# Hybrid decoder layer, gate/up stage: chunk 7's parts made at chunks 0 and 1 with one accumulating DMA, and the next block's sums put ahead of the mixing

## The chip, the cores and the metric

One NeuronCore of a Trainium2 chip runs the kernel alone. The metric is the device time of one execution in microseconds (us), lower is better. PE is TensorE, DVE is VectorE, ACT is ScalarE, POOL is GpSimd and SP is SyncE, whose queue issues most loads.

## The reference, cut to what matters

One layer on 256 tokens of width 2048: token mixing by head groups, then a dense SwiGLU feed-forward part and a final norm. All weights are float32. The part in question is the last but one line:

```python
    x = x + y @ w_out
    h = rms_norm(x, ffn_norm)
    return x + (jax.nn.silu(h @ w_gate) * (h @ w_up)) @ w_down
```

w_gate and w_up are 2048 x 5632 each, w_down is 5632 x 2048.

## The kernel before, in words

**Products.** Each float32 operand is split into a high part (rounded to float32r by a ScalarE copy) and a low part (VectorE: value less high part). A product is three matmuls: high by high, high by low, low by high. Each matmul has a 128x128 stationary tile and 512 columns.

**Chunks.** The weights are worked off in chunks of 1 MB, 128 partitions by four blocks of 512 columns. The gate/up stage has 11 blocks (FS) of 8 chunks (FB): a block makes 512 columns of gate and of up for both token halves, which gather in four PSUM banks. Chunks 1, 3, 6 and 7 are plain: 24 matmuls. Chunks 0, 2, 4 and 5 (SUMS) use a Winograd form of 2 by 2 blocks with seven products instead of eight: 21 matmuls. For it VectorE makes four sums of blocks, t_sum (three instructions, L1231 to L1236), ScalarE their high parts t_hi (L749) and VectorE their low parts t_lo (L1244), besides w_hi and w_lo of three blocks. There are two buffers of t_sum, t_hi and t_lo, used in turn. The seven products gather in seven banks; behind chunk 5, the last of them, the extra banks are mixed into the four: ScalarE copies one (L864), VectorE makes three sums (mix_sums) and then adds to two banks (mix_banks half 0) and subtracts from the other two (half 1). PE resumes into these banks with chunk 7.

**Ring and order.** All chunks but chunk 7 go through a ring of four raw buffers; w_lo is written over raw. SP loads a chunk when the one four places before it is used (chunk_used). ScalarE and VectorE prepare a chunk AHEAD = 3 chunks before PE takes it, in an order written out by hand in ffn(): at step p the chunk p + 3 is prepared. Both engines run that list in order, so a wait in it holds all that is behind it.

**Chunk 7 (BY_DMA).** It goes round the ring. SP loads it into d_raw (L407) when the block before is done (in block 0: when x is saved and normed, behind the load of chunk 5). ScalarE copies it to d_hi (L845) and writes -d_hi over it as d_lo (L848), at step 2, in block 0 at step 3. POOL then adds the weights from HBM to d_lo by an accumulating DMA (L480), which gives the low part without VectorE. d_raw and d_lo are the same memory.

**Hidden values.** At step 7 ScalarE applies Silu to the gate banks and VectorE multiplies by up (L1417). PE transposes the result at the next block's chunks 0 and 1 (hidden_turn, L1533), both times into bank 3, and ScalarE keeps each half in hid (keep_hidden, L818). The second transposition waits for the first half to be kept, the last side of chunk 1 for the second.

**Down stage.** 44 chunks (2 x DQ), with the same forms; the first three are prepared within the last gate/up block (down_hi, down_lo), with the hidden values' high and low parts xo_hi and xo_lo and four sums of them in sf.

Of the kernel before, what the change touches and what calls it, by code (L numbers as in the profile page):

```python
# [7 lines left out]
F32 = mybir.dt.float32  # L8
# [116 lines left out]
def build(nc, t):  # L125
    with ExitStack() as ctx:
# [45 lines left out]
        sf = at("sf", 144 * K, [4, P])  # L172
# [259 lines left out]
        def _(pool):  # L432
# [53 lines left out]
        def _(act):  # L486
# [327 lines left out]
            def keep_hidden(i, banks):  # L814

                for u in range(2):
                    act.wait_ge(turned, i * 2 + (u - 1))
                    nc.scalar.activation(hid[:, bass.ds(i * 4 + (2 * u - 4), 2), :].rearrange("p a b -> p (a b)"),  # L818
                                         bank[banks[u]], ACT.Copy).then_inc(hid_kept, 1)
# [5 lines left out]
            def down_hi(m):  # L825

                r, q = ring(DN0 + m), m % DQ
                slot = r % 4
                act.wait_ge(raw_in[slot], 16 * (r // 4 + 1))
                blocks = slice(1, 4) if q in DSUMS else slice(0, 4)  # L830
                nc.scalar.activation(w_hi[slot][:, blocks, :], raw[slot][:, blocks, :], ACT.Copy).then_inc(hi_ready, 1)  # L831
                act.wait_ge(hid_kept, 2 * FS if q >= DQ - 2 else 2 * FS - 2)
                nc.scalar.activation(xo_hi[m % 4][:, 0:4, :].rearrange("p a b -> p (a b)"),
                                     hid[:, 2 * q:2 * q + 2, :].rearrange("p a b -> p (a b)"), ACT.Copy).then_inc(xo_split, 1)
                if q in DSUMS:
# [4 lines left out]
                    nc.scalar.activation(xo_hi[m % 4][:, 4:8, :], sf[:], ACT.Copy).then_inc(xo_split, 1)  # L840

            def prep_apart(i):

                act.wait_ge(d_in, 16 * (i + 1))
                nc.scalar.activation(d_hi[:], d_raw[:], ACT.Copy).then_inc(d_hi_made, 1)  # L845
                act.wait_ge(d_hi_made, i + 1)
                for half in (slice(0, 2), slice(2, 4)):
                    nc.scalar.activation(d_lo[:, half, :], d_hi[:, half, :].bitcast(F32), ACT.Copy,  # L848
                                         scale=-1.0).then_inc(negated, 1)
# [51 lines left out]
            for m in range(2 * DQ):  # L901
                h, q = divmod(m, DQ)
                if m == 0:
                    keep_hidden(FS, (3, 3))
                    act.wait_ge(chunk_used, DN0)
                    act.dma_start(fnorm[:], t["final_norm"].partition_broadcast(P)).then_inc(fnorm_in, 16)
# [28 lines left out]
        def _(dve):  # L935
# [279 lines left out]
            def prep_lo(i, q, parts="sl"):  # L1215
# [11 lines left out]
                if "s" in parts:  # L1227
                    dve.wait_ge(raw_in[slot], 16 * (r // 4 + 1))
                    if p == SUMS[-1]:
                        dve.wait_ge(chunk_used, i * FB + (FF0 + SUMS[1] + 1))  # L1230
                    nc.vector.tensor_tensor(t_sum[s][:, 0:2, :], raw[slot][:, 1:3, :],  # L1231
# [4 lines left out]
                    nc.vector.tensor_tensor(t4, t2, b21, ALU.add).then_inc(sum_step, 1)  # L1236
                if "l" not in parts:
                    return
                dve.wait_ge(sum_step, i * (3 * NS) + (3 * done + 3))
                dve.wait_ge(hi_ready, r + 1)  # L1240
                nc.vector.tensor_tensor(w_lo[slot][:, 1:4, :], raw[slot][:, 1:4, :], w_hi[slot][:, 1:4, :].bitcast(F32),  # L1241
                                        ALU.subtract)
# [5 lines left out]
            for n in range(G0, FF0):  # L1248
# [12 lines left out]
                if n + AHEAD >= FF0:  # L1261
                    prep_lo(0, n + AHEAD - FF0, "s" if n == FF0 - 1 else "sl")
                elif n != MID:
                    low(n + AHEAD)
# [89 lines left out]
            def down_lo(m):  # L1354
# [3 lines left out]
                x = hid[:, 2 * q:2 * q + 2, :].rearrange("p a (t c) -> p (a t) c", t=TOK)  # L1358
                if q not in DSUMS:
# [3 lines left out]
                    dve.wait_ge(xo_split, m + down_sums_before(m) + 1)  # L1363
                    nc.vector.tensor_tensor(xo_lo[m % 4][:, 0:4, :], x, xo_hi[m % 4][:, 0:4, :].bitcast(F32),
# [6 lines left out]
                dve.wait_ge(raw_in[slot], 16 * (r // 4 + 1))  # L1371
                nc.vector.tensor_tensor(t_sum[s % 2][:, 0:2, :], raw[slot][:, 1:3, :],
                                        b12.unsqueeze(1).to_broadcast([P, 2, COLS]), ALU.add).then_inc(sum_step, 1)
                dve.wait_ge(sum_step, before + 1)
                nc.vector.tensor_tensor(t2, t1, b22, ALU.add).then_inc(sum_step, 1)
                dve.wait_ge(sum_step, before + 2)
                nc.vector.tensor_tensor(t4, t2, b21, ALU.add).then_inc(sum_step, 1)
                s3_s1, n2, s4 = sf[:, 0:2, :], sf[:, 2, :], sf[:, 3, :]
                dve.wait_ge(xo_split, m + s + 1)
                if s:  # L1380
                    dve.wait_ge(xo_made, DSUMS[(s - 1) % DNS] + DQ * ((s - 1) // DNS) + 1)
                nc.vector.tensor_tensor(s3_s1, x[:, 0:4:3, :], x[:, 1:2, :].to_broadcast([P, 2, P]),
                                        ALU.subtract).then_inc(xo_step, 1)
                dve.wait_ge(xo_step, 3 * s + 1)
                nc.vector.tensor_tensor(n2, sf[:, 1, :], x[:, 0, :], ALU.add).then_inc(xo_step, 1)
                dve.wait_ge(xo_step, 3 * s + 2)
                nc.vector.tensor_tensor(s4, x[:, 2, :], n2, ALU.subtract).then_inc(xo_step, 1)
                dve.wait_ge(sum_step, before + 3)
                dve.wait_ge(hi_ready, r + 1)
                nc.vector.tensor_tensor(w_lo[slot][:, 1:4, :], raw[slot][:, 1:4, :], w_hi[slot][:, 1:4, :].bitcast(F32),  # L1390
                                        ALU.subtract)
                nc.vector.tensor_tensor(xo_lo[m % 4][:, 0:4, :], x, xo_hi[m % 4][:, 0:4, :].bitcast(F32), ALU.subtract)
# [7 lines left out]
            def ffn(i, first=False, last=False):  # L1400
                for p in range(FB):
                    if p == 0 and first:
                        for j, u in enumerate(UNITS[FF0]):
                            dve.wait_ge(unit_filled, INDEX[u] + 1)
                            split_pair_lo(u, late_bank[j])
                        prep_lo(i, 2, "l")
# [13 lines left out]
                    if last and p + AHEAD >= FB:  # L1420
                        down_lo(p + AHEAD - FB)
                        if p == SUMS[-1]:
                            mix_banks(i, 1, i * FB + (FF0 + 7))
                    elif p == SUMS[-1]:
                        prep_lo(i, p + AHEAD, "s")
                        mix_banks(i, 1, i * FB + (FF0 + 7))
                        prep_lo(i, p + AHEAD, "l")
                    elif p + AHEAD != BY_DMA:
                        prep_lo(i, p + AHEAD)
# [61 lines left out]
        def _(pe_):  # L1491
# [375 lines left out]
            def ffn(i, first=False):  # L1867
                for p in range(FB):
                    if p == BY_DMA:
                        pe_.wait_ge(lo_added, 32 * (i + 1))  # L1870
# [173 lines left out]
```

## Time and profile before

| | us |
|---|---|
| median of 3 runs | 1151.44 (1151.28 to 1152.26) |
| profiled execution | 1152.47 |
| its span | 1150.7 |
| PE busy | 1098.2 (95%) |
| DVE busy | 911.0 (79%) |
| ACT busy | 653.4 (57%) |
| POOL busy | 69.8 (6%) |
| mean granted clock of PE | 0.984 |

The span is the profiled execution from its first to its last instruction. Matmuls are pipelined: one is 0.39 us long in the trace, but they start 0.227 us apart. The granted clock is a share of 2.4 GHz. The gate/up stage starts at about 387 us and the down stage at 912 us of the span.

### The profile page before, as it was taken

What the parts mean: (1) busy time and instruction counts of PE and PEld (TensorE: products, weight loads), DVE (VectorE), ACT (ScalarE), POOL (GpSimd) and SP (SyncE); (2) the same over time, 40 slices, a digit from 0 to 9 for tenths busy, and PEclk for the clock granted to TensorE, in tenths of its full rate; (3) what the DMA queues carried; (4) which work ended last, traced back from release to release, by engine and by line L of the source; (5) the groups of instructions that cost most, each with busy time, mean ns of one, the idle gap of its engine ahead of it and who ended that gap; (6) DMA issues with size and microseconds to landing.
All of it is one profiled execution on the core that took longest, in us unless ns stands there. A gap on an engine that the chain in (4) does not pass through costs nothing.

```text
span 1150.7 us, 12406 instructions
## 1 busy us (share of the span) xinstructions
PE 1098.2 (95%) x5094; PEld 906.2 (79%) x5094; DVE 911.0 (79%) x858; ACT 653.4 (57%) x650; POOL 69.8 (6%) x66
## 2 busy tenths in 40 slices
PE   9999999999999989899798998989989899999997
PEld 6888889977888768687686877868778688888886
DVE  7789577745666988778877788977888799999995
ACT  7567466657645655464545645545555566565653
POOL 0087000000000000000000000000000000000000
PEclk9999999999999999999999999999999999999999
DMA  8765535643555784665747667566576766565562
GB/s 330 283 227 191 195 104 162 200 146 111 169 193 184 248 266 165 200 202 200 219 146 203 204 187 242 187 186 209 191 219 195 229 234 200 201 197 206 194 208 110
DMA packets 52025, 228.56 MB, mean 199 GB/s; under 512 B 4480, under 2 KB 10368, under 8 KB 31744
## 3 DMA queue, kind: packets, MB, share of 16 engines
q1 hardware_dynamic: 47936, 213.84, 54.6%
q0 software_dynamic: 3168, 11.54, 5.6%
q10 hardware_dynamic: 864, 2.39, 0.6%
q8 instruction: 40, 0.66, 0.2%
q14 instruction: 17, 0.14, 0.0%
HBM read 223.56 MB, written 4.19 MB: 198 GB/s over the span
## 4 chain that ended last, share of the span: by engine, by line
PE 64%; DVE 10%; ACT 10%; DMA 9%; issue 6%; POOL 1%; SPq 0%; DVEq 0%; ACTq 0%
PE ps L1641 43%; DMA d_lo<-in_w_gu 8%; PE ps L1494 5%; PE ps L1496 5%; PE ps L1495 5%; ACT t_hi L749 4%; DVE w_lo L1221 3%; DVE t_sum L1231 2%; ACT w_hi L741 2%; PE ps L1533 2%; ACT d_hi L845 2%; DVE t_sum L1236 1%; DVE t_sum L1234 1%; ACT d_lo L848 1%; POOL d_lo L480 1%
## 5 line engine op out<-in xcount | busy, mean ns | idle before, releaser
L749 ACT ACTIVATE t_hi<-t_sum 128x2048 fp32r<-128x2048 f32 x44 | 84.4, 1918 | 190.2 <-DVE t_sum L1236 190.2
L1641 PE MATMUL ps<-w_hi,xp_hi 128*128 128x512 f32 x396 | 157.4, 397 | 4.2 <-DVE w_lo L1221 3.6
L948 DVE TENSOR_TENSOR w_lo<-raw,w_hi 128x2048 fp32r<-128x2048 f32 (+2 forms) x42 | 87.3, 2077 | 86.6 <-ACT w_hi L492 86.6
L1641 PE MATMUL ps<-w_lo,xp_hi 128*128 128x512 f32 x396 | 154.5, 390 | 0.0
L1641 PE MATMUL ps<-w_hi,xp_lo 128*128 128x512 f32 x396 | 154.4, 390 | 0.0
L831 ACT ACTIVATE w_hi<-raw 128x2048 fp32r<-128x2048 f32 (+1 forms) x44 | 79.1, 1799 | 76.2 <-DMA raw<-in_w_dn 76.1
L1221 DVE TENSOR_TENSOR w_lo<-raw,w_hi 128x2048 fp32r<-128x2048 f32 x33 | 75.5, 2289 | 51.4 <-ACT w_hi L741 51.4
L1641 PE MATMUL ps<-w_hi,xo_hi 128*128 128x512 f32 x292 | 113.9, 390 | 0.0
L1641 PE MATMUL ps<-w_hi,xo_lo 128*128 128x512 f32 x292 | 113.6, 389 | 0.0
L1641 PE MATMUL ps<-w_lo,xo_hi 128*128 128x512 f32 x292 | 113.6, 389 | 0.0
L1244 DVE TENSOR_TENSOR t_lo<-t_sum,t_hi 128x2048 fp32r<-128x2048 f32 x44 | 100.8, 2290 | 6.4 <-ACT t_hi L749 6.4
L492 ACT ACTIVATE w_hi<-raw 128x2048 fp32r<-128x2048 f32 (+2 forms) x42 | 73.0, 1738 | 50.4 <-DMA raw<-in_w_out 25.6
L1641 PEld LDWEIGHTS ps<-w_hi,xp_hi 128*128 128x128 f32 x396 | 74.3, 188 | 23.5 <-DVE w_lo L1221 7.9
L1641 PEld LDWEIGHTS ps<-w_hi,xp_lo 128*128 128x128 f32 x396 | 74.3, 188 | 15.9
L1641 PEld LDWEIGHTS ps<-w_lo,xp_hi 128*128 128x128 f32 x396 | 74.4, 188 | 14.4
L1361 DVE TENSOR_TENSOR w_lo<-raw,w_hi 128x2048 fp32r<-128x2048 f32 x32 | 73.2, 2286 | 12.3 <-ACT w_hi L831 12.3
L1641 PE MATMUL ps<-d_hi,xp_hi 128*128 128x512 f32 x88 | 42.2, 480 | 37.9 <-DMA d_lo<-in_w_gu 37.6
L1241 DVE TENSOR_TENSOR w_lo<-raw,w_hi 128x1536 fp32r<-128x1536 f32 x44 | 77.3, 1756 | 1.1
L1641 PE MATMUL ps<-t_hi,xp_hi 128*128 128x512 f32 x176 | 68.5, 389 | 0.4 <-DVE xp_lo L1190 0.4
L1641 PE MATMUL ps<-t_hi,xp_lo 128*128 128x512 f32 x176 | 68.5, 389 | 0.0
L1641 PE MATMUL ps<-t_lo,xp_hi 128*128 128x512 f32 x176 | 68.5, 389 | 0.0
L745 ACT ACTIVATE w_hi<-raw 128x1536 fp32r<-128x1536 f32 x44 | 65.2, 1481 | 5.2 <-DMA raw<-in_w_gu 4.9
(289 smaller groups left out, 2529.6 us busy)
## 6 DMA issues: line engine op xcount, KB each, us to landing
raw<-in_w_gu SPq DMA_DIRECT2D x77, 1024.0 KB, 4.9
raw<-in_w_dn SPq DMA_DIRECT2D x44, 1024.0 KB, 4.8
raw<-in_w_i SPq DMA_DIRECT2D x21, 1024.0 KB, 4.9
raw<-in_w_out SPq DMA_DIRECT2D x16, 1024.0 KB, 5.1
raw<-in_w_in SPq DMA_DIRECT2D x12, 1024.0 KB, 5.2
d_raw<-in_w_gu SPq DMA_DIRECT2D x11, 1024.0 KB, 4.8
d_lo<-in_w_gu POOLq DMA_DIRECT2D x22, 512.0 KB, 8.2
raw<-in_w_in SPq DMA_DIRECT2D x8, 576.0 KB, 3.8
```

The source lines that it names most:

```text
L492: nc.scalar.activation(w_hi[n % 4][:, 0:k, 0:c], raw[n % 4][:, 0:k, 0:c], ACT.Copy).then_inc(hi_ready, 1)
L745: nc.scalar.activation(w_hi[slot][:, 1:4, :], raw[slot][:, 1:4, :], ACT.Copy).then_inc(hi_ready, 1)
L749: nc.scalar.activation(t_hi[s % 2][:], t_sum[s % 2][:], ACT.Copy).then_inc(tops_hi, 1)
L831: nc.scalar.activation(w_hi[slot][:, blocks, :], raw[slot][:, blocks, :], ACT.Copy).then_inc(hi_ready, 1)
L948: nc.vector.tensor_tensor(w_lo[n % 4][:, 0:k, 0:c], raw[n % 4][:, 0:k, 0:c], w_hi[n % 4][:, 0:k, 0:c].bitcast(F32), ALU.subtract).then_inc ...
L1221: nc.vector.tensor_tensor(w_lo[slot][:], raw[slot][:], w_hi[slot][:].bitcast(F32), ALU.subtract).then_inc(lo_ready, 1)
L1241: nc.vector.tensor_tensor(w_lo[slot][:, 1:4, :], raw[slot][:, 1:4, :], w_hi[slot][:, 1:4, :].bitcast(F32), ALU.subtract)
L1244: nc.vector.tensor_tensor(t_lo[s][:], t_sum[s][:], t_hi[s][:].bitcast(F32), ALU.subtract).then_inc(lo_ready, 1)
L1361: nc.vector.tensor_tensor(w_lo[slot][:], raw[slot][:], w_hi[slot][:].bitcast(F32), ALU.subtract).then_inc(lo_ready, 1)
L1494: nc.tensor.matmul(out, hi, w_h, start=start, stop=False)
L1495: nc.tensor.matmul(out, hi, w_l, start=False, stop=False)
L1641: mm = nc.tensor.matmul(out, x, wt, start=start and j + m == 0, stop=stop and 3 * j + m == n - 1, skip_group_check=resumed)
```

## The change

It moves the preparation of chunk 7. ScalarE makes d_hi at step 0 (block 0: step 1) and the negated copy one step later, between w_hi and t_hi of the chunk prepared there, in one instruction instead of two. The accumulating DMA is one of 1 MB instead of two of 512 KB. The second half of hid is kept after w_hi of chunk 3 instead of ahead of it.

At step 5, VectorE makes the next block's chunk 0 sums first, then mix_sums, then w_lo of its three blocks, then both mixing instructions, then t_lo. Before, the order was mix_sums, mixing half 0, sums, mixing half 1, w_lo, t_lo. ScalarE's w_hi of next chunk 0 comes at step 4 instead of 5. The last block does the same with down chunk 0, whose sums of hidden values go to a buffer of their own, sf_first. The new waits are on chunk 4 being used (for the t_sum buffer) and, in down chunk 2, on chunk 0's xo_lo.

```diff
+        sf_first, sf_later = at("sf_first", 132 * K, [4, P]), at("sf", 144 * K, [4, P])
...
             for i in range(FS):
-                for half in range(2):
-                    pool.wait_ge(negated, 2 * i + half + 1)
-                    pool.dma_start(d_lo[:, 2 * half:2 * half + 2, :].rearrange("p a b -> p (a b)"),
-                                   w_gu[:, FB * i + BY_DMA, 2 * COLS * half:2 * COLS * (half + 1)],
-                                   accum_op=ALU.add).then_inc(lo_added, 16)
+                pool.wait_ge(negated, i + 1)
+                pool.dma_start(d_lo[:].rearrange("p a b -> p (a b)"), w_gu[:, FB * i + BY_DMA, :],
+                               accum_op=ALU.add).then_inc(lo_added, 16)
...
                     elif p == 0:
-                        keep_hidden(i, (3, 3))
+                        keep_hidden(i, (0,))
...
-                    if last and p + AHEAD >= FB:
-                        down_hi(p + AHEAD - FB)
-                    elif p + AHEAD != BY_DMA:
-                        prep_hi(i, p + AHEAD)
-                    if p == (3 if first else 2):
-                        prep_apart(i)
+                    q = p + AHEAD
+                    if q == BY_DMA:
+                        if last:
+                            down_hi(0, "b")
+                        else:
+                            prep_hi(i, FB, "b")
+                    elif q == FB:
+                        if last:
+                            down_hi(0, "t")
+                        else:
+                            prep_hi(i, FB, "t")
+                    elif last and q > FB:
+                        down_hi(q - FB)
+                    elif q in SUMS:
+                        prep_hi(i, q, "b")
+                        if p == (2 if first else 1):
+                            apart_negated(i)
+                        prep_hi(i, q, "t")
+                    else:
+                        prep_hi(i, q)
                     if first and p == 0:
                         root(nx2, 1, D)
+                    elif p == 0:
+                        keep_hidden(i, (1,))
+                    if p == (1 if first else 0):
+                        apart_hi(i)
...
                     if p == SUMS[-1]:
+                        ahead = (lambda parts: down_lo(0, parts)) if last else (lambda parts: prep_lo(i, FB, parts))
+                        ahead("s")
                         mix_sums(i)
+                        ahead("w")
                         mix_banks(i, 0, None)
+                        mix_banks(i, 1, i * FB + (FF0 + 7))
+                        ahead("l")
```

Here "b" is w_hi of the raw blocks, "t" is t_hi, "s" the sums, "w" w_lo of three blocks and "l" t_lo.

## Rows read from the trace of the kernel before

**Rows 1.** Windows from transposition to transposition: length, PE, PEld, DVE, ACT, POOL busy, clock, DMA.
```profile
586.46:634.50 48.04, 43.99 (x190) 35.55 (x188) 39.24 (x31) 25.45 (x20) 1.73 (x2) 0.96 0.64 197
...
681.57:726.95 45.38, 42.39 (x190) 34.41 (x189) 38.65 (x31) 24.93 (x20) 1.76 (x2) 1.00 0.67 209
...
sum 475.52, PE 437.13 PEld 353.53 DVE 393.78 ACT 256.99 POOL 17.42; mean PE 43.71 PEld 35.35 DVE 39.38 ACT 25.70 POOL 1.74
```
**Rows 2.** Waits of PE, 420 to 1140 us: us in total, times, longest.
```profile
PE ps L1641 <- DMA d_lo<-in_w_gu: 37.6, 11, 5.6
PE ps L1641 <- DVE w_lo L1221: 3.6, 10, 0.4
```
**Rows 3.** Timeline of PE: start, length; 581.69 is chunk 0, 613.08 chunk 6.
```profile
581.69 0.39 PE L1641 MATMUL ps<-w_hi,xp_hi 128*128 128x512 f32 x1
...
586.46 0.60 PE L1533 MATMUL ps<-ident,gate 128*128 128x128 f32 x4
...
588.29 0.60 PE L1533 MATMUL ps<-ident,gate 128*128 128x128 f32 x4
...
613.08 0.50 PE L1641 MATMUL ps<-w_hi,xp_hi 128*128 128x512 f32 x1 [0.36 <-DVE w_lo L1221]
```
**Rows 4.** Timeline of ACT in the same block.
```profile
585.33 1.92 ACT L749 ACTIVATE t_hi<-t_sum 128x2048 fp32r<-128x2048 f32 x1 [4.12 <-DVE t_sum L1236]
587.15 0.58 ACT L818 ACTIVATE hid<-ps 128x512 f32<-128x512 f32 x1
...
589.42 1.91 ACT L741 ACTIVATE w_hi<-raw 128x2048 fp32r<-128x2048 f32 x1
...
596.26 1.92 ACT L749 ACTIVATE t_hi<-t_sum 128x2048 fp32r<-128x2048 f32 x1 [3.19 <-DVE t_sum L1236]
...
604.96 1.90 ACT L845 ACTIVATE d_hi<-d_raw 128x2048 fp32r<-128x2048 f32 x1
```
**Rows 5.** The view of the tile d_lo: landing of the accumulating DMAs.
```profile
DMA to landing us min/median/max: 5.7/8.2/12.3
```
**Rows 6.** Timeline of POOL: the second DMA of a block.
```profile
616.84 0.86 POOL L480 DMA_DIRECT2D d_lo<-in_w_gu  x1 [7.72 <-issue]
```
**Rows 7.** The view of the tile d_raw: landing of its loads.
```profile
DMA to landing us min/median/max: 4.7/4.8/6.9
```
**Rows 8.** Timeline of DVE in the same block.
```profile
581.96 0.75 DVE L1417 SCALAR_TENSOR_TENSOR gate<-ps,stats,gate 128x512 f32<-128x512 f32 x1 [0.61 <-PE ps L1641]
582.63 1.21 DVE L1231 TENSOR_TENSOR t_sum<-raw 128x1024 f32<-128x1024 f32 x1
...
587.28 2.29 DVE L1244 TENSOR_TENSOR t_lo<-t_sum,t_hi 128x2048 fp32r<-128x2048 f32 x1 [0.19 <-ACT t_hi L749]
...
612.94 0.68 DVE L1332 TENSOR_TENSOR mix<-mix,ps 128x512 f32<-128x512 f32 x1
...
614.91 0.69 DVE L1337 TENSOR_TENSOR mix<-ps,mix 128x512 f32<-128x512 f32 x1
616.17 1.23 DVE L1347 TENSOR_TENSOR ps<-ps,mix 128x1024 f32<-128x1024 f32 x1 [0.57 <-PE ps L1641]
```
**Rows 9.** The page's DMA issues: the raw loads, KB each, median us to landing.
```profile
raw<-in_w_gu SPq DMA_DIRECT2D x77, 1024.0 KB, 4.9
```
**Rows 10.** The same view from 660 to 663 us: one load beside an accumulation.
```profile
raw<-in_w_gu SPq DMA_DIRECT2D x1, 1024.0 KB, 8.9
```
**Rows 11.** Timeline of DVE in the last gate/up block, down chunk 0.
```profile
898.49 1.22 DVE L1372 TENSOR_TENSOR t_sum<-raw 128x1024 f32<-128x1024 f32 x1
...
904.33 2.28 DVE L1394 TENSOR_TENSOR t_lo<-t_sum,t_hi 128x2048 fp32r<-128x2048 f32 x1
```
**Rows 12.** Timeline of SP's queue: the first load into d_raw.
```profile
399.88 0.34 SPq L407 DMA_DIRECT2D d_raw<-in_w_gu  x1
```
**Rows 13.** Timeline of ACT in block 0: w_hi of chunk 5, ahead of d_hi.
```profile
405.52 1.47 ACT L745 ACTIVATE w_hi<-raw 128x1536 fp32r<-128x1536 f32 x1
```
**Rows 14.** The page's first line.
```profile
span 1150.7 us, 12406 instructions
```

More of the change, by code:

```diff
@@ L839, in down_hi, with apart_hi, apart_negated @@
                     act.wait_ge(xo_step, 3 * (s + 1))
-                    nc.scalar.activation(xo_hi[m % 4][:, 4:8, :], sf[:], ACT.Copy).then_inc(xo_split, 1)
-            def prep_apart(i):
+                    nc.scalar.activation(xo_hi[m % 4][:, 4:8, :], (sf_later if m else sf_first)[:], ACT.Copy).then_inc(xo_split, 1)
+            def apart_hi(i):
                 act.wait_ge(d_in, 16 * (i + 1))
                 nc.scalar.activation(d_hi[:], d_raw[:], ACT.Copy).then_inc(d_hi_made, 1)
+            def apart_negated(i):
                 act.wait_ge(d_hi_made, i + 1)
-                for half in (slice(0, 2), slice(2, 4)):
-                    nc.scalar.activation(d_lo[:, half, :], d_hi[:, half, :].bitcast(F32), ACT.Copy,
-                                         scale=-1.0).then_inc(negated, 1)
+                nc.scalar.activation(d_lo[:], d_hi[:].bitcast(F32), ACT.Copy, scale=-1.0).then_inc(negated, 1)
             def ffn(i, first=False, last=False):
@@ L1236, in prep_lo @@
                     nc.vector.tensor_tensor(t4, t2, b21, ALU.add).then_inc(sum_step, 1)
+                if "w" in parts or "l" in parts:
+                    dve.wait_ge(sum_step, i * (3 * NS) + (3 * done + 3))
+                    dve.wait_ge(hi_ready, r + 1)
+                if "w" in parts:
+                    nc.vector.tensor_tensor(w_lo[slot][:, 1:4, :], raw[slot][:, 1:4, :], w_hi[slot][:, 1:4, :].bitcast(F32),
+                                            ALU.subtract)
                 if "l" not in parts:
                     return
[L1239 to L1242, printed above, removed]
                 dve.wait_ge(tops_hi, i * NS + (done + 1))
@@ L1358, in down_lo @@
                 x = hid[:, 2 * q:2 * q + 2, :].rearrange("p a (t c) -> p (a t) c", t=TOK)
+                sf = sf_later if m else sf_first
                 if q not in DSUMS:
@@ L1370, in down_lo @@
                 before = 3 * (NS * FS + s)
[L1371 to L1377, printed above, removed]
@@ L1386, in down_lo @@
[L1386 to L1392, printed above, removed]
+                if "s" in parts:
+                    dve.wait_ge(raw_in[slot], 16 * (r // 4 + 1))
+                    if m == 0:
+                        dve.wait_ge(chunk_used, DN0 - FB + SUMS[2] + 1)
+                    nc.vector.tensor_tensor(t_sum[s % 2][:, 0:2, :], raw[slot][:, 1:3, :],
+                                            b12.unsqueeze(1).to_broadcast([P, 2, COLS]), ALU.add).then_inc(sum_step, 1)
+                    dve.wait_ge(sum_step, before + 1)
+                    nc.vector.tensor_tensor(t2, t1, b22, ALU.add).then_inc(sum_step, 1)
+                    dve.wait_ge(sum_step, before + 2)
+                    nc.vector.tensor_tensor(t4, t2, b21, ALU.add).then_inc(sum_step, 1)
+                    s3_s1, n2, s4 = sf[:, 0:2, :], sf[:, 2, :], sf[:, 3, :]
+                    dve.wait_ge(hid_kept, 2 * FS - 2)
+                    if s:
+                        dve.wait_ge(xo_made, DSUMS[(s - 1) % DNS] + DQ * ((s - 1) // DNS) + 1)
+                    nc.vector.tensor_tensor(s3_s1, x[:, 0:4:3, :], x[:, 1:2, :].to_broadcast([P, 2, P]),
+                                            ALU.subtract).then_inc(xo_step, 1)
+                    dve.wait_ge(xo_step, 3 * s + 1)
+                    nc.vector.tensor_tensor(n2, sf[:, 1, :], x[:, 0, :], ALU.add).then_inc(xo_step, 1)
+                    dve.wait_ge(xo_step, 3 * s + 2)
+                    nc.vector.tensor_tensor(s4, x[:, 2, :], n2, ALU.subtract).then_inc(xo_step, 1)
@@ new lines, in down_lo @@
+                if "w" in parts:
+                    dve.wait_ge(sum_step, before + 3)
+                    dve.wait_ge(hi_ready, r + 1)
+                    nc.vector.tensor_tensor(w_lo[slot][:, 1:4, :], raw[slot][:, 1:4, :], w_hi[slot][:, 1:4, :].bitcast(F32),
+                                            ALU.subtract)
+                    dve.wait_ge(xo_split, m + s + 1)
+                    nc.vector.tensor_tensor(xo_lo[m % 4][:, 0:4, :], x, xo_hi[m % 4][:, 0:4, :].bitcast(F32), ALU.subtract)
@@ L1393, in down_lo @@
+                if "l" not in parts:
+                    return
                 dve.wait_ge(tops_hi, NS * FS + s + 1)
@@ L1419, in ffn @@
                                                            op0=ALU.mult, op1=ALU.mult).then_inc(hid_made, 1)
-                    if last and p + AHEAD >= FB:
+                    if p + AHEAD > FB and last:
                         down_lo(p + AHEAD - FB)
[L1422 to L1428, printed above, removed]
+                    elif p + AHEAD not in (BY_DMA, FB):
                         prep_lo(i, p + AHEAD)
```

48 lines of the change are left out of this document (22 added, 26 removed).

## The prediction

> **What bounds the kernel now.** I read the page first, then the waits of TensorE (PE), then the execution cut at PE's first transposition of each gate/up block, then the order of instructions on PE, ScalarE and VectorE in one block. PE is the engine to watch: from 440 to 916 us it is busy 437.1 of 475.5 us [rows 1], and of the time it is idle behind the start of the gate/up stage 37.6 us in 11 waits is one wait, that for the accumulating DMA into d_lo, once a block, ahead of chunk 7; another 3.6 us in ten waits is for w_lo of chunk 6 [rows 2]. The reader is to see two prices in the table by block. A block takes 47.55 us on average (475.52 / 10). In the block from 681.57 PE is granted its full clock, 2.4 GHz, and is busy 42.4 us; in the one from 586.46 the mean granted clock is 0.96, because PE runs at 1.2 GHz for a few microseconds behind its stall, and it is busy 44.0 us for the same 190 instructions [rows 1]. So a stall is paid once as idle time and, in most blocks, once more as clock.
>
> What would a block take without any stall? Chunk 0 (21 matmuls) runs from 581.69 to 586.46, 0.227 us per matmul; the two groups of transpositions add some 0.45 us each, since 588.29 - 586.46 = 1.83 us holds one of them and six matmuls [rows 3]. Four chunks of 21 matmuls and four of 24 make 180 x 0.227 + 0.9 = 41.75 us. That is the floor: 5.8 us under today's block.
>
> VectorE is not far behind: 39.4 us busy a block [rows 1]. Whatever the change gives, it can't pass some 40 us a block, and the order of VectorE's work decides what is left over. So I walk one block with the new order. T = 0 is the start of chunk 7; chunk 0 starts at 5.44, the transpositions at 10.2 and 12.04, chunks 2 to 6 at 16.55, 21.3, 26.75, 31.5 and 36.3, the next chunk 7 at 41.75 if nothing waits.
>
> **The change, part by part.**
>
> *Chunk 7's parts earlier.* Today d_hi and the two halves of d_lo are made from 604.96 on, behind t_hi of chunk 5 [rows 4], and the DMAs issue there. The halves land 5.7 to 12.3 us behind their issue, and in some blocks POOL gets the second one out 7.72 us after the first [rows 5, 6]: 13 to 14.3 us (7.72 + 0.87 + 5.7) from the first issue to the last landing; with the average stall of 3.4 us PE wants them some 10 us after it. In the new order d_raw is wanted from 14.7 and was issued at 5.5, landing 4.8 us later [rows 7]. ScalarE: hid's first half to 12.4 (below), w_hi of chunk 3 (1.9) to 14.2, hid's second half to 14.8, d_hi to 16.6, w_hi of chunk 4 (1.5) to 18.0, then the negation in one instruction to 19.9. The last one takes the place of an idle wait, the 3.19 us before t_hi at 596.26 [rows 4], though not quite: t_sum is complete at 19.1, so t_hi and t_lo of chunk 4 come 0.8 us later than they could. Chunk 4 starts at 26.75 and t_lo ends at 24.0, so that costs nothing. The one DMA of 1 MB issues at 20.2. No row shows a 1 MB accumulation. I bound it by 8.2 us (a median half) from below and 14.3 us (both halves with the longest issue gap) from above [rows 5, 6], and take 12.3. It lands at 32.5, at worst 34.5, against 42 when PE asks: 7 us of cover. The stall of 3.4 us (37.6 / 11) goes entirely, the slow clock behind it (437.13 / 10 - 42.4 = 1.3 us a block) too, and the 0.36 us for chunk 6 goes as w_hi of chunk 6 no longer stands behind d_hi and the negation. The semaphore count (16 instead of 32) costs nothing.
>
> *hid's second half behind w_hi of chunk 3.* PE's second transposition only needs the first half; the second half is needed for the last side of chunk 1, at 15.7. It is kept at 14.8: 0.9 us of cover, cost nothing.
>
> *The first half of hid, where the next stall is.* With chunk 7 no longer late, VectorE has nothing to wait for there. The second mixing instruction starts 0.43 us behind PE's end of chunk 6 (that is T; the same semaphore latency as the 0.57 us of [rows 8]) and takes 1.2; t_lo of the next chunk 0 and w_lo of the next chunk 1 take 2.2 each (2.29 less the overlap with the next instruction); the gate products take 0.67 each (581.96 to 582.63) and so sums of chunk 2 start at 7.3; t_hi follows 2.70 later (582.63 to 585.33), at 10.0; hid's first half starts 1.82 later and lasts 0.58, to 12.4 [rows 4, 8]. PE asks at 12.04. So PE waits 0.45 us with latency, once a block; all later chunk times move by it: chunk 3 at 21.8, 4 at 27.2, 5 at 32.0, 6 at 36.7, next 7 at 42.2.
>
> *Next chunk 0's sums ahead of the mixing.* In the old order mix_sums (612.94 to 615.6, 2.66 us) and the first mixing instruction come first [rows 8]. In the new one, the chain ahead of chunk 7 is: w_lo of chunk 6, sums of next 0 (2.70), mix_sums (2.66), three blocks of w_lo (587.28 - 0.19 - 585.33 = 1.76 at most, 1.67 with overlap), first mixing instruction (1.23 and 0.1 latency). That is 8.35 us from the start of the sums to PE's release. The sums wait for the raw load, which SP issues when chunk 3 is used, at 27.3, so it depends on its landing, and here the earlier accumulation costs something: it now runs from 20.2 to 32.5, over the loads of chunk 6 (issued 21.9) and next 0 (27.3). A raw load takes 4.9 us in the median, but one issued inside an accumulation took 8.9 [rows 9, 10]. With chunk 6 at the midpoint of 6.3 and 8.9 its w_lo is through at 33.6. For next 0, bounds 4.9 and 8.9, I take 7.2, since the accumulation ends 5 us into it: 34.5. Then PE is released at 34.5 + 8.35 = 42.85 instead of 42.2. With 4.9 it would be released at 41.9 (VectorE then starts at 33.6) and wait for nothing; with 8.9 at 44.5. I take a block of 42.9 us.
>
> The trace's 8.9 us is the row on which this stands. The Trainium skill (DMA: Bandwidth & Descriptors, Queues, rings and completion order) says that a DMA engine takes turns between the queues that have work for it, packet by packet, whoever issued it; that speaks against moving the accumulation to where loads are on the path. By that rule a load may take twice its 4.9 us while an accumulation runs; the trace, with 8.9, agrees.
>
> *Last block.* There the sums carry those of hid as well, and w_lo the split of xo: 898.49 to 904.33 is 5.84 us where another block needs 587.28 - 0.19 - 582.63 = 4.46 [rows 8, 11]. 1.4 us more: 44.3. The added buffer sf_first and the wait of xo_lo in chunk 2 of the down stage cost nothing: the writer is ahead in VectorE's own order. From 916 us on PE never waits for long and I take this stage as it is.
>
> *Block 0.* Its d_raw load is issued at 399.9 and lands 6.9 us later, at 406.8 [rows 7, 12]. ScalarE now waits for it ahead of w_hi of chunk 5, which ran at 405.52 [rows 13]: d_hi to 408.6, w_hi to 410.1, negation to 412.0, t_hi to 413.9, t_lo to 416.2 against 414.8. PE starts chunk 5 some 1.4 us later. What it saves is the average stall and clock, 3.4 + 1.3 = 4.7: gain 3.3.
>
> **Sum.** 9 x 42.9 + 44.3 = 430.4, against 475.5: 45.1 us less, and 3.3 of block 0: 48.4. The profiled execution took 1152.5 us (its span 1150.7 [rows 14]), which gives 1104.1; the median of the runs is 1.0 us lower, so 1103.
>
> **Rivals.**
> A, nothing waits: the loads land in under 6 us and hid's first half in time. 41.75 a block and 43.1 for the last: 418.9 + block 0's 3.3 to 4.7: 61 us less, 1091. For it: my chains miss by only 0.45 and 0.65 us. Against: VectorE has 2 us of slack a block and several waits to take from it.
> B, the loads are the new wait: both take 8.9 us. Chunk 6's raw at 31.7, w_hi 33.6, w_lo 35.8, release at 44.2; next 0's at 8.9, release 44.5. Ten blocks at 44.5 and 1.4: 446.4, 29 + 3 = 32 less: 1119. For it: 8.9 is in the trace; against: the accumulation is over when the second load is half through. By the turns between queues of the Trainium skill (same page and section), a load twice as long as 4.9 us would make it 45.4 a block and 1128, an estimate; the 8.9 stays the bound of the trace.
> C, slower than before: the 1 MB accumulation lands so late that PE waits for it again. It issues at 20.2 and is wanted at 42.2; today's block is 5.8 us longer than the floor, so it decides only from about 27 us after its issue. Halves took at most 14.3 together, with the gap of 7.7 added twice 22. At 30 us a block would be 50 and the time some 1175.
> D, the change brings nothing: a new wait as long as the old one. In B's chain that takes a load of 11.9 us for next 0 (27.3 + 11.9 + 8.35 = 47.5) in each block; no load of before is known to take that. 1150.
>
> **Chances.** My forecast (1097 to 1109) 0.52, A 0.2, B 0.2, D 0.04, C 0.04. The range for 8 in 10 leaves a piece of A and the outer half of B: 1090 to 1116. Measurement tells 0.2% (2.3 us) from no change: faster 0.94, same 0.02, slower 0.04.
>
> **What would show it.** Right: no wait of PE for the DMA into d_lo; one DMA a block issued some 20 us behind chunk 7's start; granted clock 1.00 in all blocks; blocks of 42 to 43.5 us; a wait of PE under 1 us at the second transposition, on hid; one under 1 us ahead of chunk 7, on VectorE's mixing instruction; block 0's chunk 5 later by 1.4 us. Wrong: blocks over 44 us, raw loads landing in over 9 us with VectorE waiting for them ahead of the sums; or a granted clock under 1.00, which small new stalls would have to cause.

## The result, and the profile after

The changed kernel takes 1103.47 us in the median of four runs (1102.71 to 1107.73) against 1151.85 us for the kernel before in the same comparison; the ratio is 0.9584, 95% interval 0.9556 to 0.9612. The forecast was 1103. The profiled execution is the slowest of the four, 1107.73 us with a span of 1105.2, so what follows is up to 5 us on the slow side. Its mean granted clock is 0.995, that of the other three 0.998 to 0.999; over 1105 us that makes 3 to 4 us, an estimate, and so most of the difference.

The windows from transposition to transposition, cut as in [rows 1]; the columns are the same.
```profile
483.14:526.13 42.99, 42.02 (x189) 34.50 (x188) 38.98 (x31) 25.27 (x19) 0.86 (x1) 1.00 0.68 220
526.13:568.26 42.13, 42.02 (x190) 34.49 (x189) 38.90 (x31) 25.09 (x19) 0.89 (x1) 1.00 0.70 224
568.26:611.51 43.25, 42.03 (x189) 34.49 (x188) 39.16 (x31) 25.44 (x19) 0.87 (x1) 1.00 0.68 219
...
653.54:697.24 43.70, 41.99 (x190) 34.46 (x189) 39.23 (x31) 25.50 (x19) 0.86 (x1) 1.00 0.68 216
697.24:739.38 42.14, 42.02 (x189) 34.49 (x188) 38.94 (x31) 25.12 (x19) 0.88 (x1) 1.00 0.70 225
...
825.24:870.76 45.52, 43.63 (x189) 35.63 (x188) 41.23 (x35) 28.40 (x24) 0.86 (x1) 0.96 0.66 212
sum 430.69, PE 422.03 PEld 345.97 DVE 392.90 ACT 256.15 POOL 8.69; mean PE 42.20 PEld 34.60 DVE 39.29 ACT 25.61 POOL 0.87
```
Ten blocks take 430.7 us instead of 475.5. The granted clock is 1.00 in all of them but the last. But they are not equal: from the third on, a block of 42.1 us is followed by one of 43.2 to 43.7.

The waits of PE from 400 to 1100 us (us in total, times, longest) answer to [rows 2]:
```profile
PE ps L1672 <- DVE ps L1369: 8.3, 6, 1.9
PE ps L1672 <- DVE t_lo L1266: 3.0, 1, 3.0
```
The 37.6 us for the accumulating DMA and the 3.6 us for w_lo of chunk 6 are gone. In their place stand waits for VectorE's mixing ahead of chunk 7 (8.3 us in six) and one in block 0 for t_lo of chunk 5 (3.0 us).

The landings of the accumulating DMA and of d_raw, from the views of the two tiles, answer to [rows 5, 7]:
```profile
DMA to landing us min/median/max: 8.5/9.1/10.7
```
```profile
DMA to landing us min/median/max: 4.7/4.9/8.2
```
One DMA of 1 MB lands in about 9 us, less than the 12.3 us that I took, and far ahead of PE.

Where is the new wait made? First ScalarE's timeline, in a block in which PE waited:
```profile
573.82 1.49 ACT L743 ACTIVATE w_hi<-raw 128x1536 fp32r<-128x1536 f32 x1
575.19 1.92 ACT L849 ACTIVATE d_lo<-d_hi 128x2048 fp32r<-128x2048 f32 x1
576.99 1.91 ACT L747 ACTIVATE t_hi<-t_sum 128x2048 fp32r<-128x2048 f32 x1
...
588.81 1.92 ACT L739 ACTIVATE w_hi<-raw 128x2048 fp32r<-128x2048 f32 x1 [3.04 <-DMA raw<-in_w_gu]
```
Then VectorE's from there, and PE's chunk 7:
```profile
590.76 2.29 DVE L1239 TENSOR_TENSOR w_lo<-raw,w_hi 128x2048 fp32r<-128x2048 f32 x1 [2.66 <-ACT w_hi L739]
592.97 1.22 DVE L1251 TENSOR_TENSOR t_sum<-raw 128x1024 f32<-128x1024 f32 x1
...
595.56 0.68 DVE L1354 TENSOR_TENSOR mix<-mix,ps 128x512 f32<-128x512 f32 x1
...
598.14 1.75 DVE L1261 TENSOR_TENSOR w_lo<-raw,w_hi 128x1536 fp32r<-128x1536 f32 x1
599.81 2.36 DVE L1369 TENSOR_TENSOR ps<-ps,mix 128x1024 f32<-128x1024 f32 x2
```
```profile
601.18 0.47 PE L1672 MATMUL ps<-d_hi,xp_hi 128*128 128x512 f32 x1 [1.22 <-DVE ps L1369]
```
The reader is to see an unbroken chain. ScalarE waits 3.04 us for the raw load of chunk 6, w_hi starts at 588.81, and from there w_lo, sums, mix_sums, w_lo and mixing follow without a gap to PE's release at 601.18: 12.4 us. The block before has the same chain from 545.57 to 557.93, also 12.4 us, with PE hardly waiting. The difference is the load of chunk 6. In the block before it was issued at 537.46 and took 8.1 us, in the block shown it was issued at 579.59 and took 9.2 us.

### The profile page after: what moved, and what is told of

It reads as the page before. It is cut to its first block, busy times and chain, and to the rows that moved or that the text cites. A ratio compares the mean times of both kernels' runs of the same rounds, so it can differ in the third digit from the quotient of the medians.

```text
span 1105.2 us, 12406 instructions
## 1 busy us (share of the span) xinstructions
PE 1083.0 (98%) x5094; PEld 898.8 (81%) x5094; DVE 909.5 (82%) x858; ACT 652.5 (59%) x639; POOL 57.4 (5%) x55
## 3 DMA queue, kind: packets, MB, share of 16 engines
q0 software_dynamic: 1584, 11.54, 5.6%
## 4 chain that ended last, share of the span: by engine, by line
PE 82%; DMA 6%; DVE 5%; issue 3%; ACT 3%; SPq 0%; DVEq 0%; ACTq 0%
PE ps L1672 61%; PE ps L1525 5%; PE ps L1527 5%; PE ps L1526 5%; DMA raw<-in_w_gu 5%; PE ps L1564 2%; ACT w_hi L739 1%; DMA d_raw<-in_w_gu 1%; DVE mix L1356 1%; DVE t_sum L1251 1%; DVE ps L1369 1%; PE ps L1612 1%; PE ps L1789 1%; PE ps L1790 1%; PE ps L1791 1%
## 5 line engine op out<-in xcount | busy, mean ns | idle before, releaser
L1384 DVE TENSOR_TENSOR w_lo<-raw,w_hi 128x2048 fp32r<-128x2048 f32 x32 | 73.2, 2288 | 14.4 <-ACT w_hi L830 14.3
L739 ACT ACTIVATE w_hi<-raw 128x2048 fp32r<-128x2048 f32 x33 | 63.0, 1909 | 26.0 <-DMA raw<-in_w_gu 26.0
```

The costliest lines, as they stand in the source:

```text
L739: nc.scalar.activation(w_hi[slot][:], raw[slot][:], ACT.Copy).then_inc(hi_ready, 1)
L1384: nc.vector.tensor_tensor(w_lo[slot][:], raw[slot][:], w_hi[slot][:].bitcast(F32), ALU.subtract).then_inc(lo_ready, 1)
```

## The experiments

Every kernel was compared with the kernel before on the same chip; a ratio is to that kernel, with its 95% interval. The changed kernel was measured in one of these comparisons only. Where another kernel is set against it, that goes by the two ratios, and where their intervals overlap the difference is not secure.

**Only VectorE's old order.** The changed kernel with the order of step 5 put back:
```diff
-                        ahead("s")
                         mix_sums(i)
-                        ahead("w")
                         mix_banks(i, 0, None)
+                        ahead("s")
                         mix_banks(i, 1, i * FB + (FF0 + 7))
-                        ahead("l")
+                        ahead("wl")
```


> The changed kernel with VectorE's old order at step 5 (mix_sums, mixing half 0, sums of next chunk 0, mixing half 1, w_lo, t_lo); all else of the change stays. Theory of the prediction (VectorE has only some 2 us of slack a block once PE no longer waits, so its order decides): mix_sums waits for chunk 5, the sums then push t_lo of the next chunk 0 and the first half of hid back by 2 to 3 us, PE waits for t_lo ahead of chunk 0 or at the second transposition, blocks of 44.5 to 45.5 us, 1120 to 1130 us. Rival (only chunk 7's earlier parts matter, the order is free): 1102 to 1106 us.

Measured: 1125.89 us, ratio 0.977 (0.9746 to 0.9794). Blocks of 44.66 us, all alike. Its waits of PE:
```profile
PE ps L1563 <- ACT hid L816: 16.4, 10, 1.6
PE ps L1671 <- DVE t_lo L1266: 9.6, 11, 2.1
```
Time and blocks are as expected. Both waits that the theory names are there, 0.75 us ahead of each chunk 0 and 1.64 us at each second transposition. So the new order is worth 22 us once the rest of the change is in.

**Only the new order.** Chunk 7's parts as before at step 2, in two halves, and both halves of hid kept ahead of w_hi of chunk 3; the core of the edit:
```diff
-                        if p == (2 if first else 1):
-                            apart_negated(i)
...
-                    elif p == 0:
-                        keep_hidden(i, (1,))
-                    if p == (1 if first else 0):
-                        apart_hi(i)
+                    if p == (3 if first else 2):
+                        apart_hi(i)
+                        apart_negated(i)
```


> The changed kernel with chunk 7's parts where they were (step 2, block 0 step 3), two halves, and hid's halves kept together: only the new order of sums and mixing is left of the change. Theory: PE waits for the accumulating DMA as before, blocks of 47 to 48 us, 1148 to 1153 us. Rival (the order brings a part by itself): under 1140 us.

Measured: 1148.48 us, ratio 0.9965 (0.995 to 0.9981). As the theory has it, PE still waits 31.2 us in ten waits for the DMA. Alone, the order is worth 4 us, 0.35%: the longer wait covers what it gives.

**Only one DMA.** The kernel before with one negation and one DMA, at the old place:
```diff
-                for half in range(2):
-                    pool.wait_ge(negated, 2 * i + half + 1)
-                    pool.dma_start(d_lo[:, 2 * half:2 * half + 2, :].rearrange("p a b -> p (a b)"),
-                                   w_gu[:, FB * i + BY_DMA, 2 * COLS * half:2 * COLS * (half + 1)],
-                                   accum_op=ALU.add).then_inc(lo_added, 16)
+                pool.wait_ge(negated, i + 1)
+                pool.dma_start(d_lo[:].rearrange("p a b -> p (a b)"), w_gu[:, FB * i + BY_DMA, :],
+                               accum_op=ALU.add).then_inc(lo_added, 16)
```


> The kernel before with one negation and one accumulating DMA of 1 MB, at the old place. Theory as predicted (1 MB lands some 12 us after its issue, so the early place is what removes the wait): it issues near 609 in the block of the rows, lands near 621 against 618.9 wanted, PE waits 2.5 us a block, 1135 to 1145 us. Rival (the changed kernel's trace shows 1 MB landing in 8.5 to 10.7 us, so one DMA nearly suffices at the old place): wait under 1 us, 1105 to 1122 us.

Measured: 1134.57 us, ratio 0.9851 (0.9823 to 0.9878). The time falls just under the range of the theory, by other waits than it named:
```profile
PE ps L1637 <- DMA d_lo<-in_w_gu: 17.2, 11, 2.4
PE ps L1529 <- ACT hid L816: 8.7, 8, 1.6
PE ps L1637 <- DVE w_lo L1217: 2.7, 10, 0.3
```
The DMA lands in 9.4 to 11.8 us (median 11.0), so PE waits 1.6 us for it in the mean instead of 3.4. In eight of the blocks it then waits up to 1.6 us at the second transposition, which the longer stall had hidden. A third of the whole gain comes from this edit alone, and not all of it is waiting: PE's busy time fell from 1098.2 to 1089.2 us while its mean granted clock rose from 0.984 to 0.996. That is 9 of the 19.6 us by which the span fell.

**One DMA and the new order, at the old place.** The changed kernel with the edit of "only the new order", but one negation and one DMA.

> The changed kernel with chunk 7's parts at the old place (step 2, block 0 step 3) but one negation and one DMA; hid's halves kept together. It tells what the early place adds where the order and the single DMA are there. Theory: PE waits 0.7 to 2.4 us for the DMA as with the single DMA alone, but not at the second transposition; blocks of 43.2 to 44.5 us, 1112 to 1122 us. Rival (the early place is not needed any more): 1105 us or under.

Measured: 1134.07 us, ratio 0.9851 (0.9833 to 0.9869): both theory and rival missed. The order adds nothing to the single DMA. Its waits of PE, and ScalarE's timeline of one block:
```profile
PE ps L1669 <- DVE ps L1366: 22.5, 9, 3.9
PE ps L1669 <- DMA d_lo<-in_w_gu: 5.0, 2, 2.6
```
```profile
549.20 1.90 ACT L844 ACTIVATE d_hi<-d_raw 128x2048 fp32r<-128x2048 f32 x1
551.13 1.92 ACT L849 ACTIVATE d_lo<-d_hi 128x2048 fp32r<-128x2048 f32 x1
552.95 1.90 ACT L739 ACTIVATE w_hi<-raw 128x2048 fp32r<-128x2048 f32 x1
```
PE's wait ahead of chunk 7 is no longer put down to the DMA but to the mixing, some 2.3 us a block and 3.9 us in the last. w_hi of chunk 6 stands behind d_hi and the negation on ScalarE, which take 3.75 us; VectorE waits 3.26 us for it at 554.88, and the same chain of sums and mixing runs late. With this order the early place does two things: it hides the DMA, and it takes 3.75 us of ScalarE's work from ahead of w_hi of chunk 6.

**Two halves at the new place.** The changed kernel with two negations and two DMAs of 512 KB, the diff of "only one DMA" read backwards, in the changed kernel.

> The changed kernel with two negations and two accumulating DMAs of 512 KB, at the new place. If only the landing counts: the halves are all landed some 14 us behind the first issue (about 34 of T), 7 us ahead of PE; no wait for them, and the time within 3 us of 1103.5, unless the longer traffic delays the raw loads of chunk 6 and next chunk 0 further: then blocks of 43.5 to 44.5 us and 1108 to 1118 us. Rival (one DMA is needed to hide it at all): PE waits for the DMA again, over 1120 us.

Measured: 1107.8 us, ratio 0.9624 (0.9595 to 0.9653). PE doesn't wait for the DMA, which settles the rival; its waits for the mixing are 11.7 us in nine instead of 8.3 in six, and the first nine blocks average 43.24 us instead of 42.80. The time lies between the two that were expected, within 3 us of 1103.5 and 1108 to 1118. The intervals of this ratio and of the changed kernel's overlap, so the 4 us between them are not secure, and whether the longer traffic costs anything stays open.

**No accumulation.** POOL waits for the negation and only counts the semaphore up; chunk 7's low part lacks the weights.
```diff
                 pool.wait_ge(negated, i + 1)
-                pool.dma_start(d_lo[:].rearrange("p a b -> p (a b)"), w_gu[:, FB * i + BY_DMA, :],
-                               accum_op=ALU.add).then_inc(lo_added, 16)
+                pool.sem_inc(lo_added, 16)
```


> The changed kernel without the accumulating DMA: POOL only counts the semaphore up, so chunk 7's low part lacks the weights (-d_hi alone); that part of the computation is left out. Theory (the accumulation's traffic delays the raw load of chunk 6, from which w_hi, w_lo, sums, mix_sums, w_lo and mixing follow in 12.4 us to PE's release at chunk 7): that load lands in about 5 us instead of 8 to 9, no wait at chunk 7, all blocks near 42.1, 1092 to 1096 us. Rival (VectorE's list itself is too long, the load is incidental): the waits at chunk 7 stay, 1101 to 1104 us.

Measured: 1095.15 us, ratio 0.9505 (0.9481 to 0.9528). Two of its windows:
```profile
524.99:566.97 41.98, 41.96 (x189) 34.49 (x188) 39.06 (x31) 25.13 (x19) 0.00 (x0) 1.00 0.59 200
818.91:861.37 42.46, 42.24 (x189) 34.41 (x188) 41.06 (x35) 28.68 (x24) 0.00 (x0) 1.00 0.59 203
```
The first nine blocks take 41.98 to 42.00 us each; the unevenness is gone. The waits of VectorE from 440 to 860 us, first of the changed kernel, then of this one:
```profile
DVE w_lo L1239 <- ACT w_hi L739: 21.8, 10, 3.1
DVE t_lo L1266 <- ACT t_hi L747: 9.8, 30, 0.6
DVE t_sum L1251 <- DMA raw<-in_w_gu: 0.3, 1, 0.3
```
```profile
DVE ps L1368 <- PE ps L1671: 13.4, 9, 1.5
DVE t_lo L1265 <- ACT t_hi L746: 9.8, 30, 0.6
```
With the accumulation, VectorE loses 21.8 us in ten waits for w_hi of chunk 6 and, but for 0.2 us, never waits for PE: its list, with these waits in it, is the bound. Without the accumulation they are gone and VectorE waits for PE. The raw load of chunk 6, which took 8.1 and 9.2 us in the two blocks above, takes 4.9 here in the one block read. So the accumulation's traffic costs the changed kernel some 8 us. The edit frees every load of it, but chunk 6's is the only one for which VectorE had lost more than 0.3 us.

**The first mixing instruction ahead of w_lo.** PE's wait at chunk 7 would lose the 1.67 us of w_lo from its chain:
```diff
                         mix_sums(i)
-                        ahead("w")
                         mix_banks(i, 0, None)
+                        ahead("w")
                         mix_banks(i, 1, i * FB + (FF0 + 7))
```


> The changed kernel with the first mixing instruction ahead of w_lo of next chunk 0 instead of behind it. Theory (PE's wait at chunk 7 is the chain from chunk 6's raw load, 12.4 us, of which w_lo takes 1.67): the chain is 10.7 us, the waits of 1.2 to 1.9 us at chunk 7 shrink to 0 to 0.2, blocks of 42.0 to 42.2 us, the last block 2 us shorter: 1093 to 1097 us. Rival (the second mixing instruction, pushed behind w_lo, is then late for the third side of chunk 7, or t_lo late for chunk 0): waits there of 1 us or more, 1101 us or over.

Measured: 1102.63 us, ratio 0.9585 (0.956 to 0.961): no gain that can be told. The waits of PE moved:
```profile
PE ps L1564 <- ACT hid L816: 5.5, 8, 1.1
PE ps L1672 <- DVE t_lo L1266: 1.6, 1, 1.6
PE ps L1672 <- DVE ps L1369: 0.6, 3, 0.2
```
The waits at chunk 7 shrink as the theory has it, but what VectorE has lost to the late load comes back at the second transposition, up to 1.1 us; neither theory nor rival had named this place, though the time is in the rival's range. VectorE's list is unbroken from w_lo of chunk 6 to the sums of the next chunk 2, on which hid waits; only the order within it changed. The last block of the profiled execution is 2.7 us shorter (42.81 instead of 45.52).

**The negation ahead of w_hi of chunk 4.** The accumulating DMA issues 1.2 to 1.4 us earlier behind the transposition.
```diff
-                        prep_hi(i, q, "b")
-                        if p == (2 if first else 1):
+                        if p == 1 and not first:
                             apart_negated(i)
+                        prep_hi(i, q, "b")
```


> The changed kernel with the negation (and so the accumulating DMA) ahead of w_hi of chunk 4 instead of behind it, 1.4 us earlier; block 0 as it is. Theory (VectorE loses 21.8 us in ten waits for w_hi of chunk 6, whose raw load is slowed by the accumulation; a part of the accumulation's traffic is moved out of that load's way): these waits shrink to 8 to 15 us in all, 1098 to 1101 us. Rival (the traffic in flight is the same and the queues share anew; or w_lo of chunk 4 comes 1 us later and VectorE loses there what it gains): 1102 to 1105 us.

Measured: 1108.67 us, ratio 0.9623 (0.9601 to 0.9645): slower than both expected, though the interval overlaps the changed kernel's. The gain of the theory did not come. VectorE's wait for w_hi of chunk 6 grew to 24.2 us and a new one of 8.0 us in ten came for w_hi of chunk 4. The accumulation now took 10.4 to 11.8 us to land. Moved earlier by this much, it is not out of the loads' way.

**Chunk 6 in halves.** w_hi and w_lo of chunk 6 are made in two halves each, so that VectorE starts 0.9 us sooner:
```diff
+                if p == 6:
+                    nc.scalar.activation(w_hi[slot][:, 0:2, :], raw[slot][:, 0:2, :], ACT.Copy).then_inc(half6_hi, 1)
+                    nc.scalar.activation(w_hi[slot][:, 2:4, :], raw[slot][:, 2:4, :], ACT.Copy).then_inc(hi_ready, 1)
+                    return
...
+                if p == 6:
+                    dve.wait_ge(half6_hi, i + 1)
+                    nc.vector.tensor_tensor(w_lo[slot][:, 0:2, :], raw[slot][:, 0:2, :],
+                                            w_hi[slot][:, 0:2, :].bitcast(F32), ALU.subtract)
+                    dve.wait_ge(hi_ready, r + 1)
+                    nc.vector.tensor_tensor(w_lo[slot][:, 2:4, :], raw[slot][:, 2:4, :],
+                                            w_hi[slot][:, 2:4, :].bitcast(F32), ALU.subtract).then_inc(lo_ready, 1)
+                    return
```


> The changed kernel with w_hi and w_lo of chunk 6 made in two halves each, so that VectorE starts on the first half 0.9 us earlier. The accumulation and the loads are as they are. Theory (VectorE has no slack behind that wait; it reaches both the mixing and the sums of chunk 2 late): the ten waits go from 21.8 to about 13 us, PE's waits at chunk 7 shrink by 0.8 us each, mean block 42.8 to 42.2, last block 0.8 less: 1096.5 to 1100 us. Rival (not VectorE's wait but something else sets the wait at chunk 7): 1102 to 1104 us.

Measured: 1100.94 us, ratio 0.9558 (0.9536 to 0.958). VectorE's wait for w_hi of chunk 6 fell to 14.0 us, PE's waits for the mixing from 8.3 to 5.6 us, the first nine blocks from 42.80 to 42.38 us in the mean. The last block, expected 0.8 us shorter, took 45.9. The waits moved as expected, but the time is 0.9 us above the expected range, and its interval overlaps the changed kernel's, so the 2.5 us of gain are not secure by themselves.

**Block 0.** d_hi goes behind w_hi of chunk 5 and the negation behind t_hi, in block 0 alone:
```diff
                         prep_hi(i, q, "b")
-                        if p == (2 if first else 1):
+                        if first and p == 2:
+                            apart_hi(i)
+                        elif not first and p == 1:
                             apart_negated(i)
                         prep_hi(i, q, "t")
+                        if first and p == 2:
+                            apart_negated(i)
```


> The changed kernel with block 0's d_hi behind w_hi of chunk 5, and its negation behind t_hi of chunk 5, so that ScalarE doesn't wait for d_raw ahead of either; all other blocks as they are. Theory (the 3.0 us wait ahead of chunk 5 in block 0 comes from d_raw landing 8.2 us behind its issue): that wait falls to 0.5, PE waits up to 0.7 us for the DMA instead, 1100.5 to 1102 us. Rival (the following blocks give it back): 1103 to 1104 us.

Measured: 1103.17 us, ratio 0.9581 (0.9563 to 0.9599), the same as the changed kernel. The wait ahead of chunk 5 fell to 0.45 us, as expected, but 1.17 us came ahead of block 0's chunk 7, for the mixing and not for the DMA. No gain can be told. The theory took the wait of 3.0 us for a fixed cost, and other profiles of the unchanged block 0 show that it isn't one: it follows the landing of the first d_raw load, which differs from execution to execution. First the changed kernel's window behind that wait, then the same place in the kernel with the first mixing instruction ahead of w_lo:
```profile
417.92:422.00 4.08, 4.08 (x12) 3.25 (x13) 4.01 (x4) 1.39 (x2) 0.00 (x0) 0.63 1.02 259
```
```profile
417.05:421.05 4.00, 4.00 (x17) 3.30 (x18) 3.97 (x3) 1.40 (x2) 0.00 (x0) 1.00 0.97 229
```
In the changed kernel's profile d_raw landed in 8.2 us, PE waited 3.01 us, the granted clock behind it was 0.63, and the first transposition came at 440.07. In the other d_raw landed in 6.8 us, PE waited 1.64 us, the clock stayed at 1.00, and the transposition came at 437.63; chunk 6 in halves gives 6.8, 1.66 and 436.96. The edits of both come behind that wait. Here, with 6.8 us again, it came at 437.49: no earlier than in those two.

**Both together.** Chunk 6 in halves and block 0's edit in one kernel.

> Chunk 6 in halves together with block 0's d_hi behind w_hi of chunk 5 and its negation behind t_hi. If both are right they add: 1094 to 1099 us. If block 0's gain is given back by the next blocks' waits, as its median with three rounds (1103.2 against 1103.5) would have it, it is that of the halves alone within 1 us.

Measured: 1098.88 us (1098.35 to 1098.97), ratio 0.9536 (0.9523 to 0.9549). This is within the range for two gains that add, and 2 us below the halves alone; their intervals overlap, so that the two add is not shown. Two windows of it, and its waits of PE:
```profile
437.46:479.20 41.74, 41.74 (x189) 34.58 (x188) 38.56 (x32) 24.67 (x20) 0.87 (x1) 1.00 0.70 227
479.20:522.18 42.98, 42.26 (x189) 34.43 (x188) 39.61 (x32) 25.93 (x20) 0.86 (x1) 1.00 0.68 221
```
```profile
PE ps L1689 <- DVE ps L1386: 4.8, 5, 1.4
PE ps L1689 <- DVE t_lo L1283: 0.5, 1, 0.5
PE ps L1689 <- DMA d_lo<-in_w_gu: 0.4, 1, 0.4
```
This is the fastest of the kernels that leave nothing out: 4.6 us under the changed kernel in the medians, with intervals of the ratios that don't overlap. Every second block takes 41.74 us, the floor that the prediction worked out.

## Why the prediction was right

*The floor of 41.75 us* holds: 41.74 to 41.76 us in five blocks of the last kernel, 42.0 in the one without accumulation.

*What goes away.* The wait for the DMA and the 0.36 us for chunk 6 went entirely, as forecast. So did the slow clock behind the DMA's wait: PE's busy time in the ten blocks fell by 15.1 us (437.13 to 422.03), where 1.3 us a block had been forecast. But the slow clock came back behind two new waits, in the last block and in block 0. The 1 MB DMA took 8.5 to 10.7 us where I took 12.3 and had 14.3 as the upper bound; with that much cover it made no difference to the sum.

*The wait at chunk 7* was forecast as 0.65 us in each block and is 0 or 0.8 to 1.9 us; the first nine blocks average 42.80 against the forecast 42.9. The chain behind it was sized well, but I laid the wait on the load of next chunk 0, expected at 34.5 behind the start of chunk 7. In the trace that load is there in time (ScalarE waits until 591.26, 33.3 us behind 557.93, and VectorE comes to it at 592.97), and the load of chunk 6, which I had expected at 29.5, is there at 29.8 or 30.9. From there the chain is 12.4 us. The 7.6 us taken for it, the middle of two bounds, were 0.5 to 1.6 us too few, and the 7.2 us for the other 0.7 to 1.0 us too many. So the mechanism, the accumulation over the loads, was right, and the term was put to the wrong one of two loads. The kernel without accumulation shows both: no such wait, and blocks of 42.0.

*The wait of 0.45 us at the second transposition* did not come. I had the mixing's second instruction start 0.43 us behind PE's start of chunk 7 and everything up to the sums of chunk 2 follow. In the trace the two mixing instructions run back to back and t_lo starts at 602.07, 0.9 us behind chunk 7, where I had 1.6. The three kernels in which VectorE runs later (the old order, the single DMA alone, mixing ahead of w_lo) do show that wait, up to 1.6 us: the place was right, the margin was mis-sized by 0.7 us.

*The last block* was forecast at 44.3 us and took 45.5. Its wait is 1.89 us, and behind it the clock was below full (0.96 over the block), some 1.6 us by PE's busy time (43.63 against 42.0), which I had not priced. Without the accumulation the block took 42.46 us.

*Block 0* was forecast to gain 3.3 us. Its first transposition is at 440.07 against 440.51 before, so in this profile it gained 0.4. Two terms failed. The landing of d_raw took 8.2 us instead of 6.9, and the wait ahead of chunk 5 became 3.0 us in the place of 0.5, where 1.9 had been forecast. And the slow clock behind such a wait was put at nothing: the mean granted clock from there to the transposition is 0.92, about 1.8 us. The profiled execution was also 0.5 us behind on its way there. In the two profiles with d_raw landing in 6.8 us the wait was 1.6 to 1.7 us at full clock, and the transposition came 2.9 and 3.6 us earlier than before: there the forecast of 3.3 holds.

*The sum.* The span fell by 45.5 us, 44.8 in the ten blocks (forecast 45.1), 0.4 in block 0 and 0.3 from the down stage; the median by 48.4. That the median was met to half a microsecond is partly luck: the loads' terms missed in both directions, and block 0 can gain 0.4 or over 3 us. The profiled execution was 4 us above the median; the other three have no trace, so which terms were shorter in them is not known beyond their higher clock.

*The rivals.* Nothing waits (A) is what the kernel without accumulation shows, with blocks of 42.0 instead of 41.75 us and 1095 us instead of 1091. Late loads (B) were half right: loads of 8.1 and 9.2 us there are, but only chunk 6's; in the two blocks read the next one took 6.5 and 6.2. Slower (C) and no gain (D) fall.

How the change's three edits share the gain, in medians: one DMA alone 17 us, the order alone 4, both 17; with the early place added 48, without the order 26. Most of it is in no edit by itself: each takes one wait, and the next in line is nearly as long. The early place alone, with two halves and the old order, was not run.

## What to carry to other kernels

When a wait of the bounding engine goes, walk one period in the new order on every engine with its measured durations; the waits that were hidden behind the old one decide the gain. An edit that is worth 4 us alone may be worth 22 when the others are in, so a single edit that measures little is not yet refuted. A transfer that is moved to where nobody waits for it can still delay the load that someone does wait for: look up what is in flight over its new place, and which engine has no slack behind it. One profile is one execution: in block 0 the landing of a single load moved the next stage by 3 us.

## What the runs showed of the hardware that was not expected

A 1 MB accumulating DMA takes less than two of 512 KB: 8.5 to 10.7 us from issue to landing in the changed kernel, and 9.4 to 11.8 at the old place, against up to 12.3 for one half of a pair, or some 14 us from the first issue where POOL issued the second half over 7 us late. The page of the profile counts half the packets on that queue (1584 instead of 3168) and the same share of the engines' time, 5.6%.

A raw load beside the accumulation took 8.1 and 9.2 us instead of 4.9. The Trainium skill (DMA: Bandwidth & Descriptors, Queues, rings and completion order) says that a DMA engine takes turns between the queues that have work for it, packet by packet. It gives no time for this; an estimate from it is up to twice 4.9 us, and the trace agrees with 8.1 and 9.2.

The same accumulation issued 1.2 to 1.4 us earlier took 10.4 to 11.8 us itself and left VectorE with more wait for the load, not less; why is open.

The granted clock was below full in the last block after a wait of 1.9 us (0.56 from 858.83 to 862.50), while before the change two blocks with waits of 2.6 us kept 1.00, such as that of 681.57 to 726.95 [rows 1].

Why every second block of the changed kernel waits is not settled. The chain from the load of chunk 6 is the same 12.4 us in both kinds, and the load's 8.1 or 9.2 us makes the difference; what makes the load alternate was only seen to need the accumulation. PE's waits are not what makes it: with the old order, where the blocks are all alike, w_hi of chunk 6 still starts by turns 21.7 to 22.1 and 22.3 to 23.0 us behind the transposition.
